# Two-layer hybrid encoder on one core: gate loads, top-k, rotation, convolution and linear attention put in another order

## The reference

```python
u = h @ w_in                                    # h = rmsnorm(x); 2592 columns and 4 x 1024 gate columns
oa = global_attention(qa, ka, va)               # qa, ka normed and rotated
ob = conv_module(ub, dw, dwb, lng, lnb)         # depthwise, 31 taps, then layer norm and silu
oc = window_attention(qc, kc, vc, sink)         # qc, kc rotated
od = gla_mixer(qd, kd, vd, rd, zlr, g2, gb2, gn)
gates = jax.nn.sigmoid(gates.reshape(B, S, N_BRANCH, D_MODEL))
for i, o in enumerate((oa, ob, oc, od)):
    merged = merged + gates[:, :, i] * (o @ w_branch[i])
x = x + merged @ w_out
# expert-choice mixture, 16 experts: each takes its top cap = 2 * N / 16 tokens (64 and 32)
gate, idx = lax.top_k(aff.T, cap)
ye = (silu(xe @ wg) * (xe @ wu)) @ wd * gate    # xe = hf[idx]; added back at idx
x = x + sigmoid(rmsnorm(x) @ w_ple_gate) * (p @ w_ple_proj)
```

## Time and profile before

| | |
|---|---|
| median of 3 runs | 3069.91 us |
| profiled execution | 3069.4 us, of which the span of its instructions 3067.6 us |
| TensorE busy | 2867.7 us, 93% of the span |
| VectorE, ScalarE, GpSimd busy | 1979.9, 1681.3, 331.4 us |
| mean granted TensorE clock | 0.966 of full speed |
| chain that ended last | TensorE 71%, ScalarE 10%, VectorE 8%, issue 5%, transfers 2% |

### The profile page before, as it was taken

One profiled execution on the slowest core, in us unless ns is written; L12 is line 12 of the kernel. 1 busy time (PEld: TensorE's weight loads), 2 busy tenths in 40 slices (PEclk: granted clock), 3 DMA queues, 4 the chain that ended last, 5 costly groups with the idle time before them and its releaser, 6 DMA issues.

```text
span 3067.6 us, 44335 instructions
## 1 busy us (share of the span) xinstructions
PE 2867.7 (93%) x15324; PEld 2317.2 (76%) x15324; DVE 1979.9 (65%) x2556; ACT 1681.3 (55%) x2328; POOL 331.4 (11%) x304
## 2 busy tenths in 40 slices
PE   7999999989969999997999989999898799999978
PEld 7998877878846666665789978778787566666656
DVE  4146964447378888887541669543554788888874
ACT  3223345234358888887432233442433688888874
POOL 1030000014001000110010300000330100101000
PEclk9999999999789999999999999999997899999989
DMA  5122222156469999999230222221654799999981
GB/s 179 35 64 61 61 73 66 49 156 206 172 207 375 372 374 374 374 370 355 96 85 24 76 61 61 73 61 47 188 176 165 260 375 375 375 370 375 371 309 48
DMA packets 374924, 605.31 MB, mean 197 GB/s; under 512 B 19952, under 2 KB 140496, under 8 KB 374672
## 3 DMA queue, kind: packets, MB, share of 16 engines
q1 hardware_dynamic: 360992, 557.00, 52.4%
q0 software_dynamic: 12080, 40.32, 5.1%
q10 hardware_dynamic: 1728, 6.29, 0.5%
HBM read 546.91 MB, written 56.62 MB: 197 GB/s over the span
## 4 chain that ended last, share of the span: by engine, by line
PE 71%; ACT 10%; DVE 8%; issue 5%; DMA 2%; DVEq 2%; ACTq 0%; SPq 0%; POOLq 0%; POOL 0%
PE PS L1723 17%; PE PS L1694 14%; PE PS L1696 14%; PE PS L1695 14%; ACT whi L783 5%; PE PS L1674 3%; DVE wlo L1183 1%; PE PS L1817 1%; DVE zacc L1330 1%; PE PS L2032 1%; ACT L783 1%; ACT L1090 1%; PE PS L1941 1%; PE PS L1907 1%; PE PS L1806 1%
## 5 line engine op out<-in xcount | busy, mean ns | idle before, releaser
L1183 DVE TENSOR_TENSOR wlo<-raw,whi 128x1024 fp32r<-128x1024 f32 (+2 forms) x872 | 1023.6, 1215 | 466.4 <-ACT whi L783 459.9
L783 ACT ACTIVATE whi<-raw 128x1024 fp32r<-128x1024 f32 (+2 forms) x872 | 885.3, 1044 | 372.5 <-PE PS L1696 336.5
L1723 PE MATMUL PS<-hT,fhi 128*128 128x512 f32 (+1 forms) x2048 | 452.7, 343 | 6.4 <-ACT fout L801 3.9
L1694 PE MATMUL PS<-whi,xeT 128*96 128x512 f32 x1024 | 411.9, 402 | 12.8 <-DVE wlo L1183 10.3
L1696 PE MATMUL PS<-whi,xeT 128*96 128x512 f32 x1024 | 405.7, 396 | 0.0
L1695 PE MATMUL PS<-wlo,xeT 128*96 128x512 f32 x1024 | 403.6, 394 | 0.0
L1694 PE MATMUL PS<-whi,hT 128*128 128x432 f32 (+1 forms) x960 | 359.8, 375 | 7.3 <-DVE hT L1193 5.9
L1723 PEld LDWEIGHTS PS<-hT,fhi 128*128 128x128 f32 x2048 | 318.1, 190 | 53.9 <-issue 9.8
L1696 PE MATMUL PS<-whi,hT 128*128 128x432 f32 (+1 forms) x960 | 356.3, 371 | 0.0
L1695 PE MATMUL PS<-wlo,hT 128*128 128x432 f32 (+1 forms) x960 | 356.2, 371 | 0.0
L1723 PE MATMUL PS<-hT,flo 128*128 128x512 f32 (+1 forms) x1024 | 264.9, 340 | 0.0
(11 more groups left out here) (273 smaller groups left out, 3838.6 us busy)
## 6 DMA issues: line engine op xcount, KB each, us to landing
raw<-in_w_gate_e SPq DMA_DIRECT2D x256, 512.0 KB, 10.1
raw<-in_w_up_e SPq DMA_DIRECT2D x256, 512.0 KB, 10.5
raw<-in_w_down_e SPq DMA_DIRECT2D x256, 512.0 KB, 10.3
raw<-in_w_in SPq DMA_DIRECT2D x64, 512.0 KB, 4.3
raw<-in_w_in SPq DMA_DIRECT2D x48, 432.0 KB, 3.5
gate_logits<-raw SPq DMA_DIRECT2D x32, 384.0 KB, 2.7
gate_logits<-fout SPq DMA_DIRECT2D x32, 384.0 KB, 2.7
gates<-gate_logits SPq DMA_DIRECT2D x32, 384.0 KB, 5.0
```

What stands on the lines that cost most here:

```text
L783: A(whi[slot % SPLIT][:, 0:w], raw[slot][:, 0:w], ACT.Copy).then_inc(s_hi, 1)
L1183: V.tensor_tensor(wlo[j % SPLIT][:, 0:w], raw[j % slots][:, 0:w], whi[j % SPLIT][:, 0:w].bitcast(F32), ALU.subtract).then_inc(s_lo, 1)
L1694: nc.tensor.matmul(out, x[0], w[0], start=first, stop=False)
L1723: m = nc.tensor.matmul(PS[:, bb, 0:(t1 - t0) * 128], w[wn], x[xn](t0, t1), start=first and p == 0, stop=last and p == 2)
```

## The change

In the order of a layer:

- Rotation. The last tile's transposes come behind three k steps of gate tile `F_Z`; the convolution's input is transposed into banks 4 and 5 and no longer waits for the last low halves; gate tile `F_Z + 1` follows as a whole ahead of attention, in banks 2 and 3.
- Taps. The first 8 of the 62 stand ahead of attention's first unit, the other 54 are spread over the same 36 units.
- Convolution. The output is transposed two tiles to a bank (`conv_out`), signalled two at a time; gate tile `F_CONV + 1` goes to banks 4 and 5. `gate_evicted` waits for the tile before only where it had the same bank.
- First pass. In each tile the first branch transposes come two k steps sooner, and ACT copies them ahead of the gate's eviction.
- Second pass. Its first decay products wait for ACT's last reads, not for the scan; the scan is waited for where the states are read.
- Merge. `load_gates(0)` moves up to gate tile 30, behind the last decay product (`la` is moved onto the gates' buffer), `load_gates(1)` ahead of the last store; weight step 3 is split behind the first sigmoids, not ahead of them.
- `warm` issues an activation on one unread column, ahead of the two norms and of the router's exponential.
- Top-k. The first group's 512 scores are cut into two rows of 256 at partitions 0 and 32, the second group moves to partition 64; the two descending lists of 64 are merged by comparing one with the other reversed.

```diff
@@ -78,2 +78,3 @@
 
+NTAP = 8
 F_UNITS = [n for n in range(44) if n >= 16 or n % 2 == 0]
...
@@ -247,3 +249,6 @@
         lsm = moe("lsm", [128, NT])
-        scores = moe("scores", [48, SEQ])
+        scores = moe("scores", [64 + NE, DEC])
+        upper = moe("upper", [NE, 2, CAPP])
+        lower = moe("lower", [NE, CAPP])
+        first = moe("first", [NE, CAPP])
         pick = moe("pick", [NE, 2, CAP])
...
@@ -318,3 +323,3 @@
         m_at[0] = M0
-        la = mix("la", [128, NT, 512])
+        la = at("la", [128, NT, 512], M0 + 4 * 8192)
         kvs = mix("kvs", [128, 2 * NT, 4, HD])
...
@@ -469,3 +475,7 @@
 
-            return 6
+            return {F_Z + 1: 2, F_CONV + 1: 4}.get(f, 6)
+
+        def gate_evicted(l, f):
+
+            return l * NF + f + (1 if gate_bank(f) == gate_bank(f - 1) else 0)
 
@@ -552,2 +562,7 @@
                         load_gate(f + FRAW)
+                    if f == F_GLB + NT - 1:
+                        for n in range(2):
+                            sp.wait_ge(s_fout[n], l * (8 * NF) + 2 * 16)
+                        sp.wait_ge(s_h[0], l * NT + NT)
+                        load_gates(0)
                     if f == NF - 1:
@@ -556,6 +571,4 @@
                             load_branch(g)
-                        sp.wait_ge(s_fout[0], l * (8 * NF) + 8 * NF)
-                        sp.wait_ge(s_fout[1], l * (8 * NF) + 8 * NF - 16)
-                        sp.wait_ge(s_h[8], l * NT + NT)
-                        load_gates(0)
+                        sp.wait_ge(s_od, 2 * l + 2)
+                        load_gates(1)
                     sp.wait_ge(s_fev, l * NF + f + 2)
@@ -563,5 +576,2 @@
 
-                sp.wait_ge(s_fused, l * NF + NF + FSPLIT)
-                sp.wait_ge(s_od, 2 * l + 2)
-                load_gates(1)
                 for n in range(2):
@@ -802,2 +812,6 @@
 
+            def warm(function):
+
+                A(unread[:], eps1[:], function)
+
             def mean_square(t):
@@ -932,8 +946,10 @@
                         z0 = PAD + m * 128 + (PAD if m >= 4 else 0)
-                        A(zT[:, :, z0:z0 + 128], PS[:, m % 2, 0:256].rearrange("p (c n) -> p c n", c=2),
+                        A(zT[:, :, z0:z0 + 128], PS[:, 4 + m % 2, 0:256].rearrange("p (c n) -> p c n", c=2),
                           ACT.Copy).then_inc(s_zT, 1)
-                    if t in (2, 4):
-                        gate_hi(l, F_Z + t // 2)
-                    if t in (3, 5):
-                        gate_out(l, F_Z + t // 2 - 1)
+                    if t == 2:
+                        gate_hi(l, F_Z + 1)
+                    if t == 4:
+                        gate_out(l, F_Z)
+                gate_hi(l, F_Z + 2)
+                gate_out(l, F_Z + 1)
 
@@ -1000,4 +1016,5 @@
                         gate_hi(l, F_GLA + n + 1)
+                        branch_hi(branch_units(n)[0])
                         gate_out(l, F_GLA + n)
-                        for k in branch_units(n):
+                        for k in branch_units(n)[1:]:
                             branch_hi(k)
@@ -1006,3 +1023,3 @@
                 gate_out(l, F_SCAN)
-                act.wait_ge(s_scan, l + 1)
+                act.wait_ge(s_g[8], l * NT + NT - 1)
                 for t in range(NT):
@@ -1033,3 +1050,2 @@
                 gate_out(l, F_TAIL)
-                hi(l * SPL + (S_G + 3), 3, 1024, R_G)
                 for g in range(9):
@@ -1039,4 +1055,4 @@
                             A(gates[g % 2][:, i], gates[g % 2][:, i], ACT.Sigmoid).then_inc(s_sg, 1)
+                    hi(l * SPL + (S_G + g + 3), g + 3, 1024, R_G)
                     if g >= 1:
-                        hi(l * SPL + (S_G + g + 3), g + 3, 1024, R_G)
                         act.wait_ge(s_mg, l * 8 + g)
@@ -1050,2 +1066,3 @@
 
+                warm(ACT.Sqrt)
                 for t in range(2):
@@ -1064,2 +1081,3 @@
                     act.dma_start(h2_d[t * 128:(t + 1) * 128, :], h2b[:, t, :]).then_inc(s_h2, 16)
+                warm(ACT.Exp)
                 act.wait_ge(s_lm, l + 1)
@@ -1333,2 +1356,4 @@
 
+                for k in range(NTAP):
+                    tap(k)
                 for n in range(51):
@@ -1354,3 +1379,3 @@
                         i = F_UNITS.index(n)
-                        for k in range(2 * CONVW * i // 36, 2 * CONVW * (i + 1) // 36):
+                        for k in range(NTAP + (2 * CONVW - NTAP) * i // 36, NTAP + (2 * CONVW - NTAP) * (i + 1) // 36):
                             tap(k)
...
@@ -1506,3 +1531,3 @@
                 branch_lo(11)
-                for n in range(1, 4):
+                for n in range(1, 3):
                     lo(l * SPL + (S_G + n), n, 1024)
...
@@ -1562,4 +1587,5 @@
                 dve.wait_ge(s_scz, l + 1)
-                V.tensor_copy(scores[0:NE, :], PS[0:NE, 3, :])
-                V.tensor_copy(scores[32:32 + NE, 0:DEC], PS[0:NE, 2, 0:DEC])
+                for h in range(2):
+                    V.tensor_copy(scores[32 * h:32 * h + NE, :], PS[0:NE, 3, h * DEC:(h + 1) * DEC])
+                V.tensor_copy(scores[64:64 + NE, :], PS[0:NE, 2, 0:DEC])
                 dve.drain()
@@ -1573,6 +1599,15 @@
                     dve.drain()
-                V.tensor_copy(pick[:, 0, 0:CAPP], topi[0:NE, :])
-                V.tensor_copy(pick[:, 1, 0:CAPP], top[0:NE, :])
-                V.tensor_scalar(pick[:, 0, CAPP:CAP], topi[32:32 + NE, 0:CAPS], float(SEQ), None, ALU.add)
-                V.tensor_copy(pick[:, 1, CAPP:CAP], top[32:32 + NE, 0:CAPS])
+
+
+                V.tensor_copy(upper[:, 1, :], top[32:32 + NE, ::-1])
+                V.tensor_scalar(upper[:, 0, :], topi[32:32 + NE, ::-1], float(DEC), None, ALU.add)
+                V.tensor_copy(lower[:], topi[0:NE, :])
+                V.tensor_scalar(pick[:, 0, CAPP:CAP], topi[64:64 + NE, 0:CAPS], float(SEQ), None, ALU.add)
+                V.tensor_copy(pick[:, 1, CAPP:CAP], top[64:64 + NE, 0:CAPS])
+                dve.drain()
+                V.tensor_tensor(first[:], top[0:NE, :], upper[:, 1, :], ALU.is_ge)
+                V.tensor_tensor(pick[:, 1, 0:CAPP], top[0:NE, :], upper[:, 1, :], ALU.max)
+                V.tensor_copy(pick[:, 0, 0:CAPP], upper[:, 0, :])
+                dve.drain()
+                V.copy_predicated(pick[:, 0, 0:CAPP], first[:].bitcast(I32), lower[:])
                 dve.drain().then_inc(s_pick, 1)
@@ -1730,3 +1765,3 @@
                     pe.wait_ge(s_flo, l * NF + f + 1)
-                    pe.wait_ge(s_fev, l * NF + f + 1)
+                    pe.wait_ge(s_fev, gate_evicted(l, f))
                 for k in range(k0, k1):
...
@@ -1761,2 +1795,4 @@
                         gate_step(l, F_ROPE + t)
+                    elif t == NT - 1:
+                        gate_step(l, F_Z, 0, 3)
                     for kind, r, made, low, done in (("A", rA, s_rA, s_lA, s_tA), ("C", rC, s_rC, s_lC, s_tC)):
@@ -1770,8 +1806,5 @@
                         m.then_inc(done, 1)
-                pe.wait_ge(s_lA, l * NT + NT)
-                pe.wait_ge(s_lC, l * NT + NT)
-
                 for t in range(NT):
                     if t in (2, 4):
-                        gate_step(l, F_Z + t // 2 - 1)
+                        gate_step(l, F_Z, (3, 6)[t // 2 - 1], (6, KT)[t // 2 - 1])
                     pe.wait_ge(s_zr, l * NT + t + 1)
@@ -1780,5 +1813,8 @@
                     for c in range(2):
-                        m = nc.tensor.transpose(PS[:, t % 2, c * 128:(c + 1) * 128],
+                        m = nc.tensor.transpose(PS[:, 4 + t % 2, c * 128:(c + 1) * 128],
                                                 u[:, t, UB + c * 128:UB + (c + 1) * 128], ident)
                     m.then_inc(s_zt, 1)
+                pe.wait_ge(s_lA, l * NT + NT)
+                pe.wait_ge(s_lC, l * NT + NT)
+                gate_step(l, F_Z + 1)
 
@@ -1804,2 +1840,4 @@
                             pe.wait_ge(*pt_done(l, m - 2))
+                        else:
+                            pe.wait_ge(s_fev, l * NF + F_Z + 3)
                         for k in range(nk):
@@ -1830,4 +1868,6 @@
                     for c in range(2):
-                        m = nc.tensor.transpose(PS[:, t, c * 128:(c + 1) * 128], zacc[:, c, a0:a0 + 128], ident)
-                    m.then_inc(s_zb, 1)
+                        o = t % 2 * 256 + c * 128
+                        m = nc.tensor.transpose(PS[:, t // 2, o:o + 128], zacc[:, c, a0:a0 + 128], ident)
+                    if t % 2:
+                        m.then_inc(s_zb, 2)
                 gate_step(l, F_CONV, 1, KT)
@@ -1873,4 +1913,5 @@
                     if n < NT:
-                        gate_step(l, F_GLA + n, 0 if n else 3, KT)
+                        gate_step(l, F_GLA + n, 0 if n else 3, 6)
                         branch_transposes(branch_units(n)[0])
+                        gate_step(l, F_GLA + n, 6, KT)
                     else:
@@ -1896,3 +1937,3 @@
 
-                pe.wait_ge(s_scan, l + 1)
+                pe.wait_ge(s_g[6], l * NT + NT)
```

(4 more changed lines are left out.)

15 lines of the change are left out of this document (9 added, 6 removed).

## The result

The changed kernel takes 2997.73 us (median of 4 runs, 2991.56 to 3002.76) beside 3071.36 us (4 runs, 3069.9 to 3074.6) for the kernel before. The ratio is 0.976, with a 95% interval of 0.9745 to 0.9776. The profiled execution took 2999.09 us, which is 70.3 us less than that of before.

A forecast was written before the change was run, and what follows sets the result against it. TensorE was taken as the bound, busy 2867.7 of 3067.6 us, with each vanished wait counted whole. The terms summed to 67.9 us, less 3 for unplaced waits: 65 off 3069, giving 3004 us, range 2990 to 3028.

The forecast's parts named there:

- Merge, 23.2: Merge: 18.6 us of waits caused by ScalarE standing before weight step 3, plus 4.6 of low-clock aftermath, go; ends 12 and 23.
- Top-k, 11.6: Top-k: half the columns save 6.5 us, the tail costs 0.7, copies even; net 5.8 a layer; ends -1.4 and 13.
- my sign: Top-k: a sign of being right was TensorE's wait behind it at 11 to 12 us in place of 22.8.
- Rotation, 13.3: Rotation: 14.3 us of waits get cover, less 1.0 for a new wait before the first maximum; ends 10 and 15.
- The 14.3 that I added: Rotation: TensorE waits of 4.9 (convolution's input), 4.9 (`klA`), 2.5 (`zT`) and 2.0 us (evicted gate tile).
- Attention, 5.3: Attention: eight waits of 0.66 us for the exponential go with fewer two-tap units; the 2.06 ones stay; ends 0 and 6.6.
- rival (2): Attention: the low clock, costing 5.2 us a layer, goes too, giving 2994 us; chance 0.12.
- Convolution, 3.9: Convolution: own banks end gate tiles' waits for eviction, 3.9 us; pairing's later start stays hidden; ends 2 and 4.
- First pass, 4.6: First linear-attention pass: two k steps cover six waits of branch transposes, together 4.6 us; ends 3 and 4.6.
- Scan, 3.4: Scan: of 6.9 us waiting, 1.7 a layer won; some 3 us of idle time remain; ends 0 and 5.
- Warm, 2.6: Behind the experts: only the third warm helps, hiding a 1.28 us table load in each layer; ends 0 and 5.
- the 3 that I took off: Whole kernel: 3 us subtracted from the summed gain for new small waits that could not be placed.

## Why the prediction was right, point by point

- **Merge, 23.2: right.** 23.3 in the stage, 23.3 from the edit alone on the kernel before, and the transfer is worth nothing that the time shows.
- **Top-k, 11.6: 10.3.** The rounds gave 6.3 for the 6.5, the tail costs 1.0 for the 0.7, the copies cost 0.2 where I had them even. The cost goes by the column, with a part that does not shrink (0.42 us for half the columns of 0.69). TensorE's wait is 13.6 and not the 11 to 12 of my sign.
- **Rotation, 13.3: 15.4.** As waits it was nearly exact: TensorE's idle time in the stage fell by 13.4. The 14.3 that I added all went. The new wait in front of the first maximum, for which I subtracted 1.0, did not come (TensorE has no idle time there), but the waits behind `klC` grew by as much, from 0.9 to 1.8. The wrong term was the one that I left out, the clock: in layer 2 the kernel before ran at the low level behind the 2.99 us for `klA`, and the kernel after did not.

```profile
1773.00:1777.00 4.00, 4.00 (x16) 3.44 (x15) 1.23 (x1) 1.17 (x2) 0.00 (x0) 0.57 0.02 4
```

- **Attention, 5.3: 8.1.** The eight waits that I priced went, 5.4 us of them. But waits behind the one of 2.06 grew, in layer 1 from 0.51 to 0.78 and 1.02, so that only 3.7 us of waiting went (3.9 of idle time). I took the waits that stay as fixed, and they are not. The stage gained more than that because of the clock, which gave about 2.9 (8.0 and 7.7 us at the low level before, 3.1 and 6.8 after); 1.3 I can't place. So the mechanism held and the size was off in two directions: rival (2), the low clock in attention, which I had as an alternative, came true in part. The stage without taps ahead shows that the gain belongs to the taps.
- **Convolution, 3.9.** The evictions that return with one pair of banks are 3.9 us of waiting. But the pairing of the tiles did not stay hidden as I had it: a wait for POOL stands behind the convolution now, 1.0 in this execution and 0.2 or none in four runs with the same order there, so the idle time won is 2.9 at the least. I name the pairing as its cause by its place alone; no run tests it.
- **First pass, 4.6: right as a wait,** 4.6 by the run that undoes it, and up to 8.2 with the clock.
- **Scan, 3.4.** In layer 1 it was 540.37 - (537.34 - 3.42) = 6.45 us from the start of the wait to the next gate step, and is 523.98 - 519.07 = 4.91 from the decay products to it: 1.5 won for my 1.7, and 1.4 in layer 2. But hardly any waiting went (6.9 to 6.0, both layers); what went is that the decay products ran at the low clock behind the wait, 3.59 us, and now run ahead of it in 1.89. The "3 us of idle time" that I said would remain was for both layers (6.9 less 3.4); measured it is 3.02 in each. So the size came out and the step was wrong: I had the wait cut in half, and it only moved. The run that moved the low halves won it.
- **Convolution, first pass and scan together: 11.9, measured 12.4.** Of the 12.4, 8.3 are idle time, and about 3.9 are the clock, for which I had only what the scan's rows contain. That the sum is so near is luck in part. The two undone parts give 6.1 and 8.2 us, more than that together, because a stretch at the low clock behind the scan in layer 1 is in both of these executions. It is also in the one with the last taps moved, so it isn't shown to belong to either edit.
- **Warm, 2.6: right,** 2.65 by the waits, 2.6 by the part of the chain that the load stood in. The Trainium skill, page "ScalarE: Activation LUTs", section "What ACT_TABLE_LOAD costs", puts a drain of 1.38 us beside the load; the run without the warms has the load 0.05 us behind the instruction ahead of it and the root right behind the load, so nothing of the kind is seen here. The 1.28 us a layer of difference leave no room for it.
- **Nothing for the input projection and the router norm: wrong in this pair of executions,** +6.0 and -4.3. The last section shows that both stages vary by as much from execution to execution. (The 0.95 us a layer that TensorE waited at the first rotated heads did go with the change; it lies at the end of the projection, and I had no term for it.) With the gather's 0.7 they make 2.4 of loss, near the 3 that I took off for waits I could not place. That is luck: these were no new waits.

So the 65 us of the forecast are 70.3 in the profiled executions, mostly because attention and rotation were mis-sized by 5 us in all, and more of that is clock than waiting: I had priced the waits at their bare length. The rest of the way to 2998 is that the profiled execution of the changed kernel lies 1.4 us above its median.

## What to carry to other kernels

When the engine that binds waits behind an engine that itself stands idle, look for the instruction at which that second engine stands: what is queued behind it and does not need it can go ahead, and this one reordering was worth more (23 us) than the earlier transfer, the banks and the top-k together (0, 9 and 10). Take a wait away by giving the bound engine work from elsewhere, not by shifting the other engine's load to the neighbouring unit: in the stage itself the first won 4.2 us, by the medians some ten, where the second won 0.6 in the stage and one to three by the medians. (The first also moved another wait further down the list, and neither part was tried alone.) And for the largest waits of a list that is otherwise full, expect that more than their length may be at stake: with the taps, the banks, the first pass and the scan of layer 2 more came or went than the waits, and the clock was low for longer where they stood. It is not certain for one wait: behind the 3.02 us for the low halves the clock fell in layer 2 and not in layer 1.
